# A feed-forward block with split weights: the down tile of the group ahead moved between the gate tile and the value tile

## The reference, cut to what matters

```python
D_MODEL, D_FF = 1024, 2816

def half_ffn(x, g, w_up, w_down):
    a, b = jnp.split(rmsnorm(x, g) @ w_up, 2, axis=-1)
    return x + 0.5 * ((jax.nn.silu(a) * b) @ w_down)

xp = half_ffn(xp, norm_ffn1[l], w_ffn1_up[l], w_ffn1_down[l])   # and xs
...                                                             # the mixing stage
xp = half_ffn(xp, norm_ffn2[l], w_ffn2_up[l], w_ffn2_down[l])   # and xs
```

## Time and profile before

| | us |
|---|---|
| median of 2 runs | 2627.53 (2626.55 to 2628.5) |
| profiled execution, its own time | 2628.58 |
| its span in the trace | 2626.8 |
| TensorE matmuls busy | 2547.8 (97%) |
| GpSimd busy | 1502.6 (57%) |
| VectorE busy | 1661.7 (63%) |
| ScalarE busy | 1106.3 (42%) |

### The profile page before, as it was taken

How to read it: one execution, slowest core, us unless ns; L and a number is a source line. 1 busy time by engine, 2 the same in 40 slices (tenths; PEclk the granted TensorE clock), 3 DMA queues, 4 the chain that set the end, 5 groups by cost and what they waited for, 6 DMA issues and landing times. The chain is left out here.

```text
span 2626.8 us, 46788 instructions
## 1 busy us (share of the span) xinstructions
PE 2547.8 (97%) x17516; PEld 2478.3 (94%) x17516; DVE 1661.7 (63%) x2925; ACT 1106.3 (42%) x2130; POOL 1502.6 (57%) x1110
## 2 busy tenths in 40 slices
PE   7999999999998999999998999998999999999998
PEld 6999999999997989999986788998999999999998
DVE  8676668666657238998635653325776667666665
ACT  5444444444445332212547764323444444444443
POOL 3988885888885111212323113413888886888884
PEclk8999999999998999999997999998999999999999
DMA  4222222222224222113223413422222322222222
GB/s 154 97 97 94 84 82 91 86 97 97 84 79 129 62 60 74 52 50 101 87 82 92 62 26 115 139 84 80 81 84 94 97 81 97 97 81 84 95 93 85
DMA packets 214944, 230.36 MB, mean 88 GB/s; under 512 B 35196, under 2 KB 192952, under 8 KB 214592
## 3 DMA queue, kind: packets, MB, share of 16 engines
q1 hardware_dynamic: 214720, 227.37, 27.6%
HBM read 200.14 MB, written 25.99 MB: 86 GB/s over the span
## 5 line engine op out<-in xcount | busy, mean ns | idle before, releaser
L719 POOL TENSOR_TENSOR f2w_lo<-f2raw,f2w_hi 128x512 fp32r<-128x512 f32 x224 | 324.5, 1448 | 96.2 <-ACT f2w_hi L616 85.2
L450 PE MATMUL f1ps<-f1xs_lo,f1w_hi 128*128 128x288 f32 x1248 | 371.1, 297 | 8.0 <-DVE f1xs_lo L444 6.6
L450 PE MATMUL f2ps<-f2xs_lo,f2w_hi 128*128 128x288 f32 x1248 | 371.6, 298 | 5.7 <-DVE f2xs_lo L444 4.3
L719 POOL TENSOR_TENSOR f1w_lo<-f1raw,f1w_hi 128x512 fp32r<-128x512 f32 x224 | 325.2, 1452 | 89.5 <-ACT f1w_hi L616 78.7
L451 PE MATMUL f2ps<-f2xs_hi,f2w_lo 128*128 128x288 f32 x1248 | 369.8, 296 | 0.0
L451 PE MATMUL f1ps<-f1xs_hi,f1w_lo 128*128 128x288 f32 x1248 | 369.0, 296 | 0.0
L452 PE MATMUL f2ps<-f2xs_hi,f2w_hi 128*128 128x288 f32 x1248 | 368.5, 295 | 0.0
L452 PE MATMUL f1ps<-f1xs_hi,f1w_hi 128*128 128x288 f32 x1248 | 367.7, 295 | 0.0
L1365 POOL TENSOR_TENSOR d_w_lo<-d_raw,d_w_hi 128x1024 fp32r<-128x1024 f32 x36 | 86.4, 2401 | 415.7 <-ACT d_w_hi L1230 415.6
L450 PE MATMUL d_ps<-xn_lo,d_w_hi 128*128 128x384 f32 x864 | 298.6, 346 | 7.1 <-POOL xn_lo L297 5.5
L451 PE MATMUL d_ps<-xn_hi,d_w_lo 128*128 128x384 f32 x864 | 293.8, 340 | 0.0
(11 more groups left out here) (384 smaller groups left out, 6772.4 us busy)
## 6 DMA issues: line engine op xcount, KB each, us to landing
f1raw<-in_w_ffn_up SPq DMA_DIRECT2D x44, 1024.0 KB, 5.1
f2raw<-in_w_ffn_up SPq DMA_DIRECT2D x44, 1024.0 KB, 5.1
f1raw<-in_w_ffn_down SPq DMA_DIRECT2D x22, 1024.0 KB, 4.9
f2raw<-in_w_ffn_down SPq DMA_DIRECT2D x22, 1024.0 KB, 4.9
d_raw<-in_w_in SPq DMA_DIRECT2D x35, 512.0 KB, 5.1
p_dram<-stage SPq DMA_DIRECT2D x24, 576.0 KB, 3.4
b_sg<-p_dram SPq DMA_DIRECT2D x16, 576.0 KB, 4.7
x_dram<-xT SPq DMA_DIRECT2D x1, 4608.0 KB, 15.5
```

Source lines behind the costliest of these rows:

```text
L450: nc.tensor.matmul(out, w_hi, x_lo, start=first, stop=False)
L719: nc.gpsimd.tensor_tensor(slot(w_lo, j), source(j), slot(w_hi, j).bitcast(F32), ALU.subtract)\
```

## The change

Only the list of tiles changes. For group g it was gate g, value g, down g - 1. It becomes gate g, down g - 1, value g, for all groups but the last, which keeps its order; the last down tile stays at the end. In group 0 there is no down tile ahead, so it is the same as well.

```diff
-    ORDER = [tile for g in range(NG) for tile in (("a", g), ("b", g), ("d", g - 1)) if tile[1] >= 0] + [("d", NG - 1)]
+    GROUP = lambda g: (("a", g), ("d", g - 1), ("b", g)) if g < NG - 1 else (("a", g), ("b", g), ("d", g - 1))
+    ORDER = [tile for g in range(NG) for tile in GROUP(g) if tile[1] >= 0] + [("d", NG - 1)]
```

## The result

The changed kernel takes 2822.38 us (2818.0 to 2826.75, two runs) against 2627.53: a ratio of 1.073 with the interval [1.0713, 1.0747], 7.3% slower. The prediction was 2758 with a range to 2800, so the direction was right and the size was not: 131 us forecast, 195 measured.

A forecast was written before the change was run, and what follows sets the result against it. TensorE, its matmuls busy 97% of the span, was taken as the bound. Waits 105.4, group 1 of the first halves 7.9 and clock 17.3 make 130.6 us; 2628.6 + 130.6 - 1.05 = 2758 us, range 2708 to 2800.

The forecast's parts named there:

- What bounds the kernel; nothing to gain.: TensorE never waits in the steady part; reordering can gain at most 7 us per block, twice, and can lose much more.
- Lead of the hidden tile, 36 places.: From value tile's end until its down tile asks for low halves: 35.1 us before, 11.16 after, at 36 places.
- The wait, 3.10 us.: At down tiles TensorE arrives at 11.16 us but GpSimd's last low half allows 14.26: 3.10 us, at 34 places.
- The measured neighbourhood with one collision (2.40): Group 0's value tile followed by group 1's gate tile, second half: a down tile next would have waited 2.40 us.
- Group 1 of the first halves.: Normalisation still on VectorE: wait of 5.5 us, less an old wait of 1.56 that should go; net 3.9, twice.
- The other moved waits.: ScalarE's copy of the value tile's first bank, banks for gate tiles, weight loads and later splits: nothing added.
- The clock.: Lower clock after a wait costs 1.44 us at a third of 36 places: 17.3 us, bounds 0 and 51.8.
- Every stall restarts at the lower clock: Rival: TensorE's clock falls at every down-tile wait, adding 51.8 us to 2740.8, giving 2793 us; chance 0.15.
- no wait: Rival: GpSimd's chain takes under 8.20 us, down tiles start on time, 1.56 us waits go: 2624 us; chance 0.05.
- a short one: Rival: not all three differences meet a split and the clock holds; 2.40 us at 34 places, 2717 us; chance 0.21.
- a second one: Rival: VectorE's differences delay down-tile additions, banks come free late, 1.5 us more per place, over 2810 us; chance 0.06.
- What the profile would show.: About 18 waits per block at line 450, about 2.7 us, put down to f1h_lo; groups 38 us apart; clock 0.95 to 1.00.

The follow-up runs named there:

- the runs with 7 and 3 fillers: The changed kernel with 7 or 3 matmuls that nobody reads at the head of each down tile's wait: 2764.29 us and 2764.94 us.
- The run with 24 fillers: The changed kernel with 24 matmuls that nobody reads in the fourth step of 36 value tiles, far from the wait: 2844.55 us, ratio 1.0825.
- the run with the shorter wait: The changed kernel with each low half ahead of the same step's split in GpSimd's queue: 2679.65 us, ratio 1.0187.
- that with 14 fillers: The changed kernel with 14 matmuls that nobody reads at the head of each down tile's wait: 2747.37 us, ratio 1.0445.
- with 12: The changed kernel with 12 matmuls that nobody reads in the fourth step of 36 value tiles, far from the wait: 2841.88 us, ratio 1.0805.

## Why the prediction was right and wrong

*What bounds the kernel; nothing to gain.* Right. With the wait removed, both orders stand within 0.3% of each other.

*Lead of the hidden tile, 36 places.* Right: 18 waits per block, at line 450, at the down product.

*The wait, 3.10 us.* Right to the digit at nearly all places, and by the parts it was made of: 10.25 us of undisturbed chain, three collisions of about 0.35, a start at +2.84 where +2.87 was forecast. The measured neighbourhood with one collision (2.40) would have misled; adding up what the new order puts beside the chain did not. The Trainium skill (GPSIMD Engine Reference, Specifications) names the shared SBUF interfaces for it, and the trace agrees by 1.15 against 0.80.

*Group 1 of the first halves.* 5.4 and 5.7 us against 5.5 forecast, and the waits of 1.56 us gone, with those of 1.38 as well.

*The other moved waits.* Right: no wait at banks, splits, differences or loads appeared.

*The clock.* This is the step that failed: "I take a third of the 36 places, 12 x 1.44 = 17.3 us, with bounds 0 and 36 x 1.44 = 51.8". It measured 85.2 us, beyond the upper bound, and was wrong twice. The share: 34 of 36 places and not 12. I held against it that dense matmuls stand on both sides; the runs with 7 and 3 fillers show falls between just such stretches. The price: 2.7 us at 28 places, where the only row that was used, gave 1.44; there the matmuls had run 3.0 us at the lower clock, here 5.9. One row is enough for an estimate but gives no upper bound. The evidence for the share was misread as well. The idle time ahead of 820.77 us was counted as one after which the clock held, from the window up to 822 us. The next windows of the kernel before show the fall:

```profile
822.00:824.00 2.00, 1.09 (x9) 1.00 (x8) 0.56 (x3) 0.23 (x2) 0.00 (x0) 0.65 0.92 174
824.00:826.00 2.00, 1.45 (x3) 0.84 (x4) 1.08 (x6) 0.27 (x1) 0.00 (x0) 0.50 1.47 581
```

So the clock fell behind all three idle times, and this one had the dense matmuls of block f1 ahead of it. Between it and the fall stand only 128x1 matmuls, so that row can't tell whether the wait or the thin work behind it was the cause; but it was no case for a clock that holds. How many of the 36 places would fall was not to be had from these three rows.

*The rivals.* "Every stall restarts at the lower clock" had 0.15 and the right mechanism; its time (2793) fell short by its price. The Trainium skill (TensorE: Matmul & The Clock Gate, HAM oscillation) tells of loops that pay at each repetition, behind waits of some 3 to 5 us; 32 of 34 equal waits agree. The run with 24 fillers doesn't, with 1 of 34 at the same idle time. The rivals of no wait, of a short one and of a second one were wrong.

*What the profile would show.* The idle time per wait was 2.94 by the profile, not 2.7, and put down to f1w_lo, not f1h_lo; the groups came 40.96 us apart, not 38; the middle of a block has 0.91, not 0.95.

## What to carry to other kernels

A producer with an average load of 57% can still be the bound of one tile: when a consumer is moved closer, list what stands ahead of the last piece in the producer's queue, with the collisions that the new order makes. A wait of TensorE has two prices, its length and the clock behind it; where waits of 2 to 3 us come at a fixed beat, take the full price (here up to 2.7 us) at every place as the upper bound. When a move exposes such a wait, first try to put the small urgent pieces ahead of the bulk work in the producer's queue, which here was worth 196 us and left nothing else to pay.

## What was not expected of the hardware

- Equal idle times of TensorE (2.93 and 2.94 us) let the clock fall at 34 of 34 places in one kernel and at 1 of 34 in another that differs by 1.3 us of matmuls per group. Idle times of 0.8 to 1.5 us never did (34 places each in the run with the shorter wait and in that with 14 fillers).
- Two kernels that did different amounts of work per group settled at almost the same beat: 40.96 us without fillers and 40.97 with 12, with 2.7 and 1.4 us lost to the clock. With 24 the beat is 40.99, with nearly nothing lost. What ties the first two to it is open.
- A stretch at the lower clock covered 5.9 us of matmuls behind a wait, 24 of them at 0.24 us in place of 0.133: nearly as much lost again as by the wait of 3.1 us itself.
- Some falls came when the wait was over: the clock went to 0.50 up to 1.5 us after matmuls had started again, so the first matmul behind a wait doesn't tell whether it cost a fall.
- Filling an idle TensorE with useless matmuls made the changed kernel 79 us faster.
